# A gated hybrid block on one core: the input projection as one level of Strassen, with a new schedule of heads

## What is computed

```python
mod = silu(c) @ w_ada + b_ada                      # shift, scale, gate
h = rms_norm(x, g_pre) * (1.0 + scale) + shift
proj = h @ w_in                                    # 1024 x 1024 @ 1024 x 6144
hq, hf, hi, hg, dq, dk, dv, dg, ma, mb = split(proj)   # 8 x 512 columns, 2 x 1024
# branch A: 4 heads of 128: a gated linear recurrence S_t = diag(f_t) S_{t-1} + (1 - f_t) i_t^T, o_t = S_t^T q_t
o_a = rms_norm(hgrn2(hq, hf, hi)) * silu(hg)
# branch B: 4 heads, two causal softmax maps of 64 dimensions each
o_b = rms_norm((softmax(q1 k1^T / 8) - lam * softmax(q2 k2^T / 8)) v) * (1 - lam_init) * silu(dg)
y = sigmoid(ma) * (o_a @ w_branch_a) + sigmoid(mb) * (o_b @ w_branch_b)
x = x + gate * rms_norm(y @ w_out, g_post)
```

## Time and profile before

| | before |
|---|---|
| runs (us) | 994.97, 989.72, 990.54; median 990.54 |
| the profiled execution | 990.12, its span 988.4 |
| mean granted clock of PE | 0.982 |
| first matmul of the projection | 46.42 |
| rounds 0 to 5 start at | 46.42, 169.13, 312.73, 456.19, 599.61, 754.90 |
| last branch product ends, gate row begins | 888.18 |
| ACT busy | 361.4 |
| moved by DMA | 59.70 MB, 60 GB/s |

### The profile page before, as it was taken

One profiled execution on the slowest core, in us unless ns is written; L12 is line 12 of the kernel. 1 busy time (PEld: TensorE's weight loads), 2 busy tenths in 40 slices (PEclk: granted clock), 3 DMA queues, 4 the chain that ended last, 5 costly groups with the idle time before them and its releaser, 6 DMA issues.

```text
span 988.4 us, 12573 instructions
## 1 busy us (share of the span) xinstructions
PE 909.9 (92%) x5025; PEld 748.8 (76%) x5025; DVE 562.0 (57%) x861; ACT 361.4 (37%) x611; POOL 194.8 (20%) x134
## 2 busy tenths in 40 slices
PE   0789899998999998999998999999999999998996
PEld 0658788786777786777886778788788888887885
DVE  2984843778567777577876567852352232325232
ACT  6840033643143743334652335744321111114111
POOL 2453122121112211121211222111211212100000
PEclk9999999998999998999998999999999999999999
DMA  9624010110001110001100010111212121024222
GB/s 355 226 94 161 23 43 22 43 44 22 22 23 42 31 35 23 23 26 39 44 23 22 23 54 22 32 32 32 65 33 75 32 64 33 29 98 151 86 86 86
DMA packets 66030, 59.70 MB, mean 60 GB/s; under 512 B 2420, under 2 KB 59828, under 8 KB 64948
## 3 DMA queue, kind: packets, MB, share of 16 engines
q1 hardware_dynamic: 65396, 58.76, 18.2%
q10 hardware_dynamic: 576, 0.13, 0.1%
HBM read 54.69 MB, written 4.19 MB: 60 GB/s over the span
## 4 chain that ended last, share of the span: by engine, by line
PE 75%; DVE 15%; ACT 4%; issue 3%; SPq 2%; DMA 1%; POOL 0%; DVEq 0%; ACTq 0%
PE pj L653 15%; PE pj L654 14%; PE pj L655 14%; PE sp L678 9%; PE by L595 3%; PE by L596 3%; PE by L597 3%; PE by L536 3%; PE by L561 3%; PE bx L530 2%; PE sp L523 1%; PE sp L522 1%; DVE acc L928 1%; DMA ada<-in_w_ada 1%; DVE cols L1011 1%
## 5 line engine op out<-in xcount | busy, mean ns | idle before, releaser
L653 PE MATMUL pj<-h_hi,w_hi 128*128 128x512 f32 x768 | 319.5, 416 | 10.5 <-POOL h_lo L384 5.3
L654 PE MATMUL pj<-h_lo,w_hi 128*128 128x512 f32 x768 | 302.4, 394 | 0.0
L655 PE MATMUL pj<-h_hi,w_lo 128*128 128x512 f32 x768 | 302.2, 394 | 0.0
L486 POOL CAST w_hi<-w_raw 128x1024 fp32r<-128x1024 f32 x48 | 56.3, 1172 | 646.2 <-PE pj L655 621.8
L653 PEld LDWEIGHTS pj<-h_hi,w_hi 128*128 128x128 f32 x768 | 146.1, 190 | 48.0 <-POOL h_lo L384 9.0
L655 PEld LDWEIGHTS pj<-h_hi,w_lo 128*128 128x128 f32 x768 | 145.8, 190 | 32.2
L654 PEld LDWEIGHTS pj<-h_lo,w_hi 128*128 128x128 f32 x768 | 146.3, 191 | 30.6 <-issue 3.8
L488 POOL TENSOR_TENSOR w_lo<-w_raw,w_hi 128x1024 fp32r<-128x1024 f32 x48 | 120.5, 2510 | 3.9
L790 ACT ACTIVATE p<-sp,cols 128x128 f32<-128x128 f32 (+7 forms) x64 | 47.4, 741 | 34.5 <-DVE cols L1012 33.8
L1085 DVE TENSOR_TENSOR f<-by,f 128x512 f32<-128x512 f32 x16 | 11.1, 691 | 80.8 <-PE by L597 80.8
L1011 DVE TENSOR_REDUCE cols<-sp 128x1 f32<-128x128 f32 (+7 forms) x64 | 48.5, 758 | 2.2
(11 more groups left out here) (194 smaller groups left out, 1398.6 us busy)
## 6 DMA issues: line engine op xcount, KB each, us to landing
w_raw<-in_w_in SPq DMA_DIRECT2D x48, 512.0 KB, 3.9
ada<-in_w_ada SPq DMA_DIRECT2D x8, 1024.0 KB, 13.4
x_in<-in_x SPq DMA_DIRECT2D x8, 512.0 KB, 5.1
ada_g<-in_w_ada SPq DMA_DIRECT2D x8, 512.0 KB, 7.7
wo_raw<-in_w_out SPq DMA_DIRECT2D x8, 512.0 KB, 5.7
res<-in_x SPq DMA_DIRECT2D x8, 512.0 KB, 4.1
out_x<-y2n SPq DMA_DIRECT2D x8, 512.0 KB, 2.8
wb_raw<-in_w_branch_a SPq DMA_DIRECT2D x8, 256.0 KB, 2.9
```

What stands on the lines that cost most here:

```text
L486: pool.tensor_copy(w_hi[j % 2][:, :], w_raw[j % 2][:, :]).then_inc(s_whi, 1)
L653: pe.matmul(pj[g % 2][:, :], wh, h_hi[:, hs], start=(kk == 0), stop=False)
L654: pe.matmul(pj[g % 2][:, :], wh, h_lo[:, hs], start=False, stop=False)
L655: last = pe.matmul(pj[g % 2][:, :], wl, h_hi[:, hs], start=False, stop=(kk == KT - 1))
```

## The change

The weights, h and the result of the projection are seen as 2 x 2 blocks: two column tiles of 128 (j), two halves of the 1024 inputs (kh), two halves of the sequence. A pair of column tiles is a group, 24 in all, four a round: (f, q), (i, hg), (dq, dk), (dv, dg), then ma and mb in pairs. The eight block products of a group, of 12 matmuls each, become seven in Winograd's form, in the order M1, M2, M6, M5, M7, M3, M4, which are 168 steps, 28 a round.

- **Weights.** SP loads four blocks of 128x512 a group. POOL makes four sums or differences of them when it comes to M6, and for each product a cast and a subtraction of 512 columns. Rings of three hold high and low parts.
- **h.** Seven panels of 128x2048 (three blocks as they are, four combinations) with high and low parts are made before or beside group 0 by DVE, ACT and POOL.
- **Results.** M1, M6, M5 go into running sums in PSUM; ACT copies after M1, M6, M5 (into snapshots) and M4 (into its place), DVE adds bank and snapshot after M2, M7, M3. Sigmoids, gates and decays follow in place: `post` on ACT and DVE.
- **Scores.** q and k stay f32; map m uses rows 64m to 64m + 63 of both, one f32 matmul (two instructions) a chunk. The low halves and their DVE subtractions go. `qk` waits for both exponentials of the tile before.
- **Schedule.** Every unit stands before a product. Attention tile i is scored at step 2i, combined at 2i + 1, transposed at 2i + 2, multiplied at 2i + 4. Levels, eight now (the two of the diagonal are one of 16 calls with 64 columns), stand at steps 9 to 16, one each; `vt` to `ssa` at 17 to 26.
- **Branches.** o_a and o_b go to DRAM a head at a time, and come back beside group 23. All 32 branch products stand behind the last projection product, alternate between `by` and `bx`, and have weights split by POOL. w_out is split beside them.
- The DMA scratch is 1024 bytes, which frees SBUF.

The diff, cut to its core:

```diff
+PAIRS = [("f", "q"), ("i", "hg"), ("dq", "dk"), ("dv", "dg")]
+M1, M2, M6, M5, M7, M3, M4 = range(PROD)
+COPIED = (M1, M6, M5, M4)
+ADDED = (M2, M7, M3)
...
+LEV_AT = {9: 0, 10: 1, 11: 2, 12: 3, 13: 4, 14: 5, 15: 6, 16: 7}
+REC_AT = {17: [("vt", 0)], 18: [("vt", 1), ("kt", 0)], 19: [("kt", 1)], 20: [("st", 0)], 21: [("st", 1)],
+          22: [("o", 0)], 23: [("o", 1)], 25: [("ssa", 0)], 26: [("ssa", 1)]}
...
+            for g in range(2, GROUPS):
+                sp_.wait_ge(s_wlo, PROD * (g - 1))
+                load_w(g)
...
+            def weights(g, m):
...
+                n = PROD * g + m
+                ring_free(n)
...
+                elif m == M6:
+                    for e in (2, 3):
+                        pool.wait_ge(s_wq[g % 2][e], 16 * (g // 2 + 1))
+                    pool.wait_ge(s_wlo, n)
+                    s2 = w_sum[n % 3]
+                    combine(a21, a11, a21, ALU.subtract)
+                    combine(s2, a22, a21, ALU.subtract)
+                    combine(a11, s2, a11, ALU.add)
+                    combine(a12, a12, s2, ALU.subtract)
+                    split(n, s2)
...
+            for m in (M1, M2, M6):
+                weights(0, m)
+            pool.wait_ge(s_mod, 1)
+            pool.wait_ge(s_xt, 2 * KT)
...
+            weights(0, M5)
...
+            pool.tensor_tensor(b_raw[M7][:, :], xq[1][1][:, :], xq[0][1][:, :], ALU.subtract).then_inc(s_t3, 1)
+            weights(0, M7)
...
+                        for m in range(2):
+                            rows = slice(64 * m, 64 * m + 64)
+                            last = pe.matmul(sp[:, m, c0:c1_], dq[rows, i * P:(i + 1) * P], dk[rows, c0:c1_],
+                                             start=True, stop=True)
...
+            def product(n):
+                g, m = divmod(n, PROD)
+                if n >= 2:
+                    if (n - 2) % PROD in COPIED:
+                        pe.wait_ge(s_pja, act_reads(n - 2))
+                    else:
+                        pe.wait_ge(s_pjd, dve_reads(n - 2))
+                pe.wait_ge(s_wlo, n + 1)
+                fresh = m in (M1, M2, M5)
...
+                dve.tensor_tensor(home(g, j, half), pj[n % 2][:, :], snap[:, :], ALU.add).then_inc(s_pjd, 1)
...
+            dve.tensor_tensor(t1[:, :], xq[0][1][:, :], xq[0][0][:, :], ALU.subtract).then_inc(s_t1, 1)
...
+            dve.tensor_tensor(t2[:, :], xq[1][1][:, :], t1[:, :], ALU.subtract).then_inc(s_t2, 1)
+            dve.wait_ge(s_t2, 1)
+            low(M6, t2)
+            low(M5, t1)
+            dve.tensor_tensor(b_raw[M4][:, :], xq[1][0][:, :], t2[:, :], ALU.subtract).then_inc(s_t4, 1)
+            low(M3, xq[1][1])
+            dve.wait_ge(s_t4, 1)
+            low(M4, b_raw[M4])
```

More of the change, by code:

```diff
@@ L168, in x_act, with tr_count @@
     return before(u, list(BANK_X))
+Y_ALL_ACT = sum(BANK_Y.get(u[0]) == "act" for u in ORDER)
+Y_ALL_DVE = sum(BANK_Y.get(u[0]) == "dve" for u in ORDER)
+X_ALL = sum(u[0] in BANK_X for u in ORDER)
+def tr_count(tiles):
+    h, i = divmod(tiles, NT)
+    return 12 * h + i + max(0, i - 4)
 def build(nc, x, c, w_ada, b_ada, g_pre, g_post, w_in, lb_logits, hg_norm_gain, lambda_q1, lambda_k1,
@@ L238, in build @@
         cols = small("cols", 256)
+        masks = [small(f"mask{n}", 64) for n in range(len(LEVELS) - 1)]
         used = [0]
@@ new lines, in _ @@
+            for n in range(4 * KT):
+                branch(n)
+                if n == 16:
+                    pe.wait_ge(s_pja, act_reads(STEPS - 1))
+                    pe.wait_ge(s_pjd, dve_reads(STEPS - 1))
+                    for e in range(KT):
+                        last = pe.matmul(pj[e // 4][:, (e % 4) * P:(e % 4 + 1) * P], gate_col[:, e:e + 1].to_broadcast([P, P]),
+                                         ident[:, :], start=True, stop=True)
+                    last.then_inc(s_gb, 1)
@@ new lines, in post @@
+                    for half in range(2):
+                        act.wait_ge(s_pjd, dve_reads(at_product(r, 0, M3 if half else M2)))
+                        act.activation(part(k, half), part(f, half), ACT.Sigmoid, scale=-1.0).then_inc(s_fp, 1)
+                        act.activation(part(f, half), part(f, half), ACT.Sigmoid).then_inc(s_fp, 1)
+                if r < HEADS and s == 15:
+                    act.wait_ge(s_pjd, dve_reads(at_product(r, 1, M7)))
+                    gate_sig(gate_a, 1)
```

1195 lines of the change are left out of this document (634 added, 561 removed).

## The result

The changed kernel takes 1044.4 us (median; 1042.7 to 1045.9), the kernel before 990.4: a ratio of 1.053 with an interval of 1.050 to 1.056, so it is slower by 54 us, and 57 above the forecast of 987. Its profiled execution has a span of 1042.9 us, to be set against the 985.1 of the sum.

A forecast was written before the change was run, and what follows sets the result against it. The prediction took TensorE, busy 92% of the span, as the bound. Its terms, 988.4 + 18.4 - 12 - 5.3 - 4.4, gave 985.1 us of span and 987 us measured, range 963 to 1011.

The forecast's parts named there:

- the sum: Whole kernel: 988.4 + 18.4 (round 0) - 12 (rounds 1 to 3) - 5.3 (rounds 4, 5, branches) - 4.4 (tail) = 985.1 us.
- The matmuls: Projection: 2304 matmuls become 2016 at 0.227 us, 65.4 us less, 10.9 a round, if nothing else ends last.
- The scores on row halves: Scores: halves run in parallel, 7.7 us and some 2 of lag a head; rival, one after the other, 1003 us, chance 0.28.
- PE's wait for POOL in round 5: Round 5: no units cover POOL's weights for M6, so each group loses 2.0 us and takes 21.1.
- the three signs of being wrong: Start ending before 90; a round under 132 or over 147 us; PE's waits for DVE in the middle not rising.
- the wait of 3.93 us with its slow clock goes: Rounds 1 to 3: PE's wait for DVE's combine of the widest tile vanishes, as tile and transposition get two longer steps.
- waiting on scores that PE itself brings late: Steps 9 to 16 of rounds 1 to 3: 3.5 us charged to DVE, within 55 us for the middle.
- not priced: Rounds: two more waits of 4 us in each, with a slow stretch behind each, would add 14 us a round; no chance given.
- 9 us of turns in the middle: Steps 9 to 16 of rounds 1 to 3: DVE charged 9 us for taking turns with POOL's 22 us there.
- the +14.3: Round 0: forecast to end at 187.5, where it ends at 169.13 in the kernel before, +18.4.
- my bound was +6: Start: modulation ready 4 us later than the 44.66 before, at 48.5, with bounds 0 and +6.
- my working of the panels: Start: DVE's 24 us and POOL's 22 exclude each other, so 45 us pass before the last panel; step 9 at 101.5.

The follow-up runs named there:

- a_qk_first: The changed kernel with the scores qk put ahead of the value product pv in PE's order within an even step: 1021.4 us, ratio 1.032 to the kernel before.
- a_pool_short: The changed kernel with POOL's weight work from group 3 on cut to 8 of 512 columns (projection wrong): 965.7 us, ratio 0.976 to the kernel before.
- a_early_out: The changed kernel with products 0 and 1 taken out of their banks amid the panels, not behind the last: 1037.0 us, ratio 1.048 to the kernel before.
- f_short_two: The changed kernel with three repairs (qk first, early copies, early first combination) and POOL's weight work from group 3 on cut to 8 columns: 946.6 us, ratio 0.953.
- b_pool_short: The kernel before with POOL's weight work from the third tile on cut to 8 of 1024 columns (projection wrong): 966.3 us, ratio 0.972.
- c_two: The changed kernel with qk ahead of pv, products 0 and 1 out early, and POOL's first combination ahead of its ring wait: 1011.0 us, ratio 1.019.

## Why the prediction was wrong

**What was right.** The matmuls: 2016, and round 5 without POOL is 28 x 2.72 = 76.2. The scores on row halves run side by side. Steps 9 to 16 and 17 to 27 of round 0 (44 and 42 us forecast, 43.5 and 42.0 measured), steps 17 to 27 of the later rounds (49, measured 48.1), branches and tail (188.3, measured 189.8). PE's wait for POOL in round 5 is there, 2.40 us for 2.0. DVE is busy over 620 us. Of the three signs of being wrong that I had named one came true: a round takes 150 us, over 147.

**The middle of rounds 1 to 3: the step that failed.** I wrote that "the wait of 3.93 us with its slow clock goes", and charged 3.5 us "for waiting on scores that PE itself brings late", 55 in all. It took 65.6. I had counted what each engine has to do and not followed one bank through PE's order: `pv` ahead of `qk`, on the bank that the last level holds. The runs put 6.7 us a round on that order (a_qk_first, 150.2 to 143.5), which is 20 of the 32 us that the three rounds came late. The case that I had left "not priced", two more waits of 4 us in a round with a slow stretch behind each, +14, was near to what happened: 10.7 us of waits in four pieces, and a round 10.7 above the forecast.

**The turns: right in kind, charged in too few places.** My charge of 9 us of turns in the middle is what a_pool_short gives back there (8 to 10 us). But I charged them in the middle alone. Steps 0 to 8 lose 5.4 us and steps 17 to 27 3.9 to POOL, and round 4 loses 8. That the forecasts of steps 0 to 8 (35 us; 36.6 up to 388.30) and 17 to 27 (49; 48.1) came near is luck: other sizes hid the error. POOL's busy time, 575 us where I said 460, has two errors. The weights of the projection take 490 us where I had 463, since POOL's waits in the turns count as its busy time too (1400 ns for a subtraction of 1270, 725 for a cast of 550). And I left out of the sum what POOL does for the branch and output weights, 57 us, and for the panels, 24.

**The start.** Of the +14.3, 4.7 are the modulation: it is ready at 53.2, 8.5 after the 44.66 of before, where my bound was +6. The sum over partitions begins 6.2 later, and it takes 3.2 more at the lower clock, which differs from execution to execution (3.92 in a_early_out). The copy of product 0 behind five panels on ACT makes 7.7, and some 2 stay open. In my working of the panels I wrote out DVE's and POOL's turns and took the ends of PE's products from them; ACT's queue was not in it.

**Round 5.** 91.6 for 84.8. The wait was 0.4 us longer in each of four groups. The rest is the clock, 0.94 in this stretch: behind three of the four waits (771 to 774, 816 to 818.5, 839.5 to 842.5) it reads 0.50, behind the one at 792.79 it stays at 1.00. I had priced the wait and not what can follow it.

**The earlier trace rows misread.** I took the 3.93 us for DVE's own work on the widest tile. Most of it was a turn with POOL's subtraction (2.92 us for 0.75). In a kernel with three times as much of POOL's work that row was the warning, and I used it as something that the change would remove.

**Where the 65 us went, then.** With the order and the start repaired and POOL's weight work short on both sides (f_short_two and b_pool_short, spans 942.9 and 965.1) 22 us are won. Round 0 ends at 192.0 against 171.6, 20.4 later where its matmuls are 10.9 less: 31 us go there, ahead of step 9, which stands at 105.8, while the earlier trace rows has the like stage begin at 81.20. POOL's turns with the panels are in these 31 us, since f_short_two keeps POOL's full work up to group 2, and no run parts them from the panels' own work. Rounds 1 to 3 take 382.3 against 405.5, 23.2 less of 32.7: 9.5 us. The rest, 2 us, lies behind them. The true kernel pays on top 64 us for POOL's work (c_two less f_short_two: turns, late weights and what the clock makes of both), and the 33 of the repairs that it lacks; the kernel before pays 27 for POOL. How the turns and the slow clock share the 64 is not fully known, as no run takes one away and leaves the other. But the loss by the clock is 42 us in c_two and 30 in f_short_two, so by an estimate from these the clock accounts for at most some 12.

## What to carry to other kernels

Before an engine is given more to do, ask which other engine it locks out, and for how long at a time; a share of busy time doesn't tell, and a partner's busy time is no proof of work. Follow each bank through the order of the engine that writes it: a unit that must wait for a bank belongs behind the one for which the other engine waits. And pauses of TensorE like these, of 1.3 to 4.4 us, are to be priced with the slow stretches that can follow them; where one can't be removed, idle work in it may even pay.

## What the runs showed of the hardware

- A DVE instruction from SBUF to SBUF waits for a whole POOL instruction, and the trace books the wait as its duration: 0.75 us becomes 2.92 (380.20 in the kernel before). A per-partition constant with one SBUF tile is hit as well (734 to 1503 ns in the mean), not only two tiles.
- The price of POOL's time rose from 0.20 to 0.34 us for each us with the load in one and the same kernel. POOL's casts, moved to ACT, gave nothing there.
- 29 us of TensorE work added made a kernel 6.9 us faster, with the granted clock up from 0.938 to 0.958.
- The 32 small matmuls of the modulation's sum took 3.63 to 3.92 us or 6.83, by the granted clock in that execution: a start that differs by 3 us without any edit.
- f32 matmuls on the two row halves overlap: 896 columns of both in 1.77 us, where one alone would need 1.50 by the earlier trace rows and the two in series 3.0.
